# Attention's rows turned one step later, with a fourth place for rows, and head 0's operands loaded ahead of a weight tile

## What is computed

```python
proj = u @ w_in                                  # xp | q | k | v | gate_logits
z = einsum('bhqd,bhkd->bhqk', qb, kb) * scale    # 8 heads of 64, 8 query blocks of 128
mask = kpos < qpos
log_beta = log_sigmoid(z)
log_1m_beta = where(mask, log_sigmoid(-z), 0.0)
log_a = log_beta + cumsum(log_1m_beta, axis=3, reverse=True) - log_1m_beta
a = where(mask, exp(log_a), 0.0)                 # the rows of weights
out = einsum('bhqk,bhkd->bhqd', a, vb)
g = sigmoid(gate_logits)                         # gates, from u @ w_in as well
m = g_pool * y_pool + g_sb * (out @ w_branch_attn)
```

## Time and profile before

| what | us |
|---|---|
| median of 3 runs | 1917.36 (1917.35 to 1918.03) |
| the profiled execution's own time | 1918.11 |
| its span | 1916.2 |
| PE busy | 1903.5 (99%) |
| PEld busy | 1592.0 (83%) |
| DVE busy | 1372.2 (72%) |
| ACT busy | 796.4 (42%) |
| POOL busy | 115.9 (6%) |

### The profile page before, as it was taken

The page is one execution under the profiler, slowest core; times in us unless marked ns, Lnnn a source line. Parts: engine busy times, 40 slices in busy tenths (PEclk is TensorE's granted clock), DMA queues, the critical chain, the costliest instruction groups (busy, mean ns, idle before and its releaser), DMA issues.

```text
span 1916.2 us, 24977 instructions
## 1 busy us (share of the span) xinstructions
PE 1903.5 (99%) x9010; PEld 1592.0 (83%) x9010; DVE 1372.2 (72%) x1677; ACT 796.4 (42%) x1175; POOL 115.9 (6%) x157
## 2 busy tenths in 40 slices
PE   9999999999999999999999999999999999999998
PEld 8888888888888888888888888898888888888887
DVE  6978777784566776488677768889777777756555
ACT  7423232323434544234676752474323232324344
POOL 1000000000000300000233220010000000000001
PEclk9999999999999999999999999999999999999999
DMA  5456654558676733416875447643545444677665
GB/s 165 144 198 230 223 181 140 199 189 306 208 240 201 195 110 132 132 50 181 226 174 148 128 139 260 197 138 119 178 144 196 149 169 153 216 264 244 206 192 206
DMA packets 258419, 348.24 MB, mean 182 GB/s; under 512 B 29344, under 2 KB 161184, under 8 KB 255008
## 3 DMA queue, kind: packets, MB, share of 16 engines
q1 hardware_dynamic: 258336, 347.15, 56.3%
HBM read 233.83 MB, written 112.99 MB: 181 GB/s over the span
## 4 chain that ended last, share of the span: by engine, by line
PE 97%; DVE 1%; DMA 1%; issue 0%; SPq 0%; ACT 0%; POOL 0%; POOLq 0%; DVEq 0%; ACTq 0%
PE bank L1263 40%; PE bank L1372 9%; PE bank L1319 9%; PE bank L1321 9%; PE bank L1320 9%; PE bank L1513 6%; PE bank L1215 3%; PE bank L1449 2%; PE bank L1421 2%; PE bank L1479 2%; PE bank L1585 2%; PE bank L1604 1%; PE bank L1190 1%; PE bank L1603 1%; PE bank L1570 1%; PE bank L1568 1%
## 5 line engine op out<-in xcount | busy, mean ns | idle before, releaser
L2253 DVE TENSOR_TENSOR dn_lo<-dn_lo_raw,dn_hi 128x1024 fp32r<-128x1024 f32 x149 | 181.9, 1224 | 149.6 <-ACT dn_hi L1788 149.1
L1263 PE MATMUL bank<-lo_t,wa_hi 128*128 128x512 f32 x656 | 252.8, 389 | 0.0
L1263 PE MATMUL bank<-hi_t,wa_hi 128*128 128x512 f32 x656 | 252.8, 389 | 0.0
L1263 PE MATMUL bank<-hi_t,wa_lo 128*128 128x512 f32 x656 | 252.8, 389 | 0.0
L1788 ACT ACTIVATE dn_hi<-dn_lo_raw 128x1024 fp32r<-128x1024 f32 x149 | 158.0, 1061 | 218.8 <-DMA dn_lo_raw<-act_dram 218.8
L1319 PE MATMUL bank<-dn_hi 128*128 128x512 f32 x596 | 232.7, 390 | 0.0
L1321 PE MATMUL bank<-dn_lo,dn_hi 128*128 128x512 f32 x596 | 231.9, 389 | 0.0
L1320 PE MATMUL bank<-dn_hi,dn_lo 128*128 128x512 f32 x596 | 231.9, 389 | 0.0
L1263 PE MATMUL bank<-hi_b,wa_hi 128*128 128x512 f32 x492 | 190.6, 389 | 1.0 <-DVE up L2387 1.0
L1263 PE MATMUL bank<-lo_b,wa_hi 128*128 128x512 f32 x492 | 190.5, 389 | 0.0
L1263 PE MATMUL bank<-hi_b,wa_lo 128*128 128x512 f32 x492 | 190.4, 389 | 0.0
(11 more groups left out here) (275 smaller groups left out, 3747.7 us busy)
## 6 DMA issues: line engine op xcount, KB each, us to landing
wa_lo_raw<-in_ffn_w_gate_up_dram SPq DMA_DIRECT2D x87, 512.0 KB, 5.0
dn_lo_raw<-act_dram SPq DMA_DIRECT2D x149, 256.0 KB, 4.2
act_dram<-g SPq DMA_DIRECT2D x44, 512.0 KB, 4.4
wd_t<-in_ffn_w_down_dram SPq DMA_DIRECT2D x44, 512.0 KB, 6.6
act_dram<-s_of SPq DMA_DIRECT2D x88, 256.0 KB, 6.5
wd_dram<-wd_t SPq DMA_DIRECT2D x22, 1024.0 KB, 6.0
dn_lo_raw<-wd_dram SPq DMA_DIRECT2D x85, 256.0 KB, 3.4
dn_lo_raw<-in_ffn_w_down_dram SPq DMA_DIRECT2D x64, 256.0 KB, 3.0
```

Of the source, the lines that this page charges most:

```text
L1263: last = nc.tensor.matmul(acc, lhs, rhs, start=n == 0 and i != 2 and i < 5, stop=n == 11, skip_group_check=True)
L2253: return nc.vector.tensor_tensor(dst, raw, hi.bitcast(f32), ALU.subtract)
```

## The change

The lag between a tile's logits and its transposes goes from two steps to three (`LAG`), with a fourth place for rows (`a3`) and one more step at the end (`DRAIN`). The weighing of pairs moves from even to odd steps. On DVE the low halves always go before the scan. The second gate unit is loaded behind head 0 instead of before it, and its four pieces are split somewhat later.

```diff
-DRAIN = 4
+DRAIN = 5
+LAG = 3
...
-    return gate_step(piece_start(j) + (7 + 18 * piece if j < NG - 1 else 1 + 6 * piece))
+    return gate_step(piece_start(j) + (20 if j == 1 else 7) + 18 * piece if j < NG - 1 else piece_start(j) + 1 + 6 * piece)
...
+        a3 = at("a3", [P, SEQ], f32, o + 16384)
...
             gate_unit(0)
             spill_pool_branch(2)
-            gate_unit(1)
...
             load_head(0)
+            gate_unit(1)
             spill_pool_branch(3)
             load_head(1)
...
-                    if s == NA:
+                    if s == NA + 1:
                         move_o(NA // 2 - 2, 3, slice(0, HALF // 2))
-                    elif s == NA + 2:
+                    elif s == NA + 3:
                         move_o(NA // 2 - 1, 4, slice(HALF // 2, HALF))
-                    elif s >= 4 and s % 2 == 0:
-                        store_o((s - 4) // 2)
+                    elif s >= LAG + 2 and s % 2:
+                        store_o((s - LAG - 2) // 2)
...
             def weights_of(n):
-                return a2[:, :] if n % 3 == 2 else a[:, n % 3, :]
+                return (a[:, 0, :], a[:, 1, :], a2[:, :], a3[:, :])[n % 4]
...
                 gate_parts(g0, cut)
-                if s >= 4 and s % 2 == 0:
-                    weigh((s - 4) // 2)
-                if 2 <= s < NA + 2:
-                    turn(s - 2)
+                if s >= LAG + 2 and s % 2:
+                    weigh((s - LAG - 2) // 2)
+                if LAG <= s < NA + LAG:
+                    turn(s - LAG)
...
                 if n >= 2:
                     act.wait_ge(a_ok, n - 1)
-                if n >= 3:
-                    act.wait_ge(t_ok, CHUNKS[n - 2])
+                if n >= 4:
+                    act.wait_ge(t_ok, CHUNKS[n - 3])
...
-                if s >= 4 and s % 2 == 0:
-                    take_o((s - 4) // 2)
-                if 2 <= s < NA + 2:
-                    turned_hi(s - 2)
+                if s >= LAG + 2 and s % 2:
+                    take_o((s - LAG - 2) // 2)
+                if LAG <= s < NA + LAG:
+                    turned_hi(s - LAG)
...
-                turned_first = 2 <= s <= NA and TILES[s - 1]["qt"] in (1, 5, 3)
-                if turned_first:
-                    turned_lo(s - 2)
+                if LAG <= s < NA + LAG:
+                    turned_lo(s - LAG)
                 if 1 <= s <= NA:
                     weigh_keys(s - 1)
-                if 2 <= s < NA + 2 and not turned_first:
-                    turned_lo(s - 2)
```

## The result

The changed kernel takes 1926.25 us (median of 5, 1925.14 to 1927.6), the kernel before 1917.63: ratio 1.0043, 95% interval 1.0032 to 1.0055. It is 8.6 us slower, where I forecast 2.2 us less. The profiled execution took 1925.14 us with a span of 1923.2, against 1918.11 and 1916.2 before. From the first gate matmul to the first of the branch the stage takes 247.8 us instead of 240.5; nothing outside it moved by more than 0.3 us.

The account below looks back on a forecast made before the run. PE, busy 99% of the span, was taken as the bound, with only waits to win: -1.4 (pipeline) - 0.9 (head 0) + 0.1 (`pool_y`) = -2.2 us, giving a median of 1915.2 us, range 1913.3 to 1918.6.

Parts of the forecast that it names:

- That only waits can be won, and which: PE in the changed stage: no matmul is removed, so only waits count, 3.6 us in all, 1.9 at head 0.
- Head 0's wait: PE's wait for head 0's late keys: loading them ahead of the weights gains 0.9 us, bounds nothing to 1.9.
- The Trainium skill's fixed cost plus bytes: Head 0's key transfers: 2.0 us plus bytes at 436 GB/s, about 2.3 us, gaining 1.9 us; rejected for the measured row.
- What stands behind the megabyte: DMA transfers after the moved weights: about 2.2 us later, `pool_y` at 926.9, charged 0.1 us, bounds 0 to 2.
- My sign of being wrong: At POOL: its wait for `pool_y` ending later than 927.4 with PE waiting at tile 2 would show the forecast wrong.
- Who waits for the mask of tile 2: POOL's mask, then DVE's scan, 2.3 us after `pool_y` lands: tile 2's transposes, in step 5, allow landing until 927.4.
- The later pieces of the second gate unit: Splitting of the moved weights on ACT: each piece a step later, claimed covered, so no cost.
- Low halves first: DVE order before the scan: two waits before weighings within the stage go, 0.3 us gained; the scan's delay costs nothing.
- One more step at the end: The stage's tail: last turning, weighing and gates keep their distances; cost 0, bounds -0.1 to +0.3 us.
- The lag: Three steps from logits to transposes, with a fourth place: PE's waits for scanned rows go, 1.1 us gained.
- scans as the bound: Rival at DVE's loop: longer than two steps for wide tiles, late `betas` stall PE; 1921.2 us or more, chance 0.10.
- a late `pool_y`: POOL's wait for `pool_y`, with later tiles' masks queued behind it: charged 0.1 us, bounds 0 to 2 us.

## Why the prediction was wrong

- **That only waits can be won, and which.** Right. Head 0's wait was forecast to fall by 0.9 us. By starts it fell from 1.77 to 0.76 us, 1.0 us; with the 0.1 us at `q_st`, which is gone too, 1.1 us. The lines are

```profile
912.15 0.39 PE L1374 MATMUL bank<-u_hi,w_lo 128*128 128x512 f32 x1
913.14 0.50 PE L1570 MATMUL bank<-k_hi,q_st 128*128 128x512 f32 x1 [0.60 <-DMA k_lo<-qk_dram]
```

The size was nearly right, the way to it less so. The transfers of keys took 2.8 to 3.5 us from issue to landing, all of them less than the 3.8 us that I had taken as the best case, and they were issued 0.2 us earlier; but PE, too, reached the second chunk 0.3 us earlier. The Trainium skill's fixed cost plus bytes ("DMA: Bandwidth & Descriptors", "Anatomy of one DMA") would have cleared the wait. The page gives it for transfers that GpSimd issues, so it was not the rule for these, which SyncE issues; the 0.76 us that stayed agrees with the row and not with that figure.
- **What stands behind the megabyte: the step that failed.** I wrote that "all behind it lands about 2.2 us later" and that `pool_y` at 926.9 was "covered by half a microsecond". It landed near 929.2, 4.6 us later. The term was worked out from bytes in the DMA engines, 3.6 us less 1.0 and 0.5 for slack. What it left out is SyncE's own queue: the issue of `pool_y` alone moved by 3.7 us, 3.2 of them the time that issuing the weights, the stores and head 1 took, and the transfer itself took 0.9 us longer. The 1.5 us that I had taken off did not show. My sign of being wrong came as written: POOL's wait ended at 929.27, later than 927.4, and PE waited, though one weighing earlier than I had said.
- **Who waits for the mask of tile 2.** The same step named only the transposes of tile 2. On DVE, low halves first means that the scan of tile 2 in step 3 stands ahead of the low halves of tile 1 in step 4, and these are wanted by the first weighing, which PE reaches before those transposes. I priced the new order within a step and did not follow it into the next. The run with the scan moved shows the two apart: 6.2 us with this link, 1.9 us without it. The later pieces of the second gate unit were priced as covered on ACT; on DVE one of them stood in this chain, for 1.7 of the 6.2 us.
- **The clock.** Not in the forecast: a stall of 6 us brought 3.2 us at 1.2 GHz, 1.35 us more.
- **Low halves first.** "The two waits before weighings within the stage go": they did not; waits of 0.29, 0.21 and 1.35 us stand in their place. At the last, near 1074 us, DVE's rows show a split and the differences of the values, together 2.9 us, right ahead of the low halves that the weighing, now in an odd step, wants:

```profile
1070.63 1.72 DVE L3050 TENSOR_TENSOR w_lo<-w_raw,w_hi 128x512 fp32r<-128x512 f32 x1
1072.28 1.21 DVE L2943 TENSOR_TENSOR v_w_raw<-v_w_raw 128x1024 f32<-128x1024 f32 x1
1073.41 1.14 DVE L3038 TENSOR_TENSOR at_lo<-bank,at_hi 128x512 fp32r<-128x512 f32 x2
```

This place was not tested by itself. In the run with later gates its wait was 0.28 us, but a wait of 0.75 us came near 1011 us, which the changed kernel does not have, and that one went when the values were moved. The causes of the 0.29 and the 0.21 us stay open.
- **One more step at the end.** Costed at 0, bounds -0.1 to +0.3 us; it cost 0.8 us. The step has five gate matmuls and no logits, so the last pair but one lost the distance that it had before. The end itself kept its balance, as forecast: the last gate at 1156.58, the branch at 1156.93.
- **The lag.** The waits for rows did go (0.45, 0.53 and 0.11 us), as forecast.

The sum by measured terms: 6.2 for the first weighing, 1.35 for the clock, 1.35, 0.8 and 0.5 for the later waits, less 1.1 at head 0 and 1.4 for the old waits: 7.7 us. The stage grew by 7.3 us in the profiled execution; the 0.4 us between them is not accounted for. The medians are 1.6 us further apart than the profiled executions. That the landing of `pool_y`, which PE now follows, differs between executions could explain this; only the profiled executions have traces, so it is not shown.

The rival that ended on the right side, scans as the bound, had the wrong mechanism: ACT waited for a scan once in the whole stage, the 5.1 us within the stall. I had a late `pool_y` as a cost of 0 to 2 us and not as a rival; its bound above was the mistake in the chances.

## What to carry to other kernels

When a load is moved, follow every queue behind it. The issuer's own queue comes first, for issuing takes time too: here it was 3.2 of the 3.7 us by which a transfer was issued late. Then follow every in-order queue behind each waiter into the following steps: here a transfer delayed one POOL instruction, and two more engines later PE stood still. Keep instructions that wait for a DMA behind those that the critical engine wants, rather than tune the DMA's arrival; putting POOL's gates two steps later took back the whole loss. A longer lag between stages is worth only as much as the shortest distance left: here it came with a new parity of steps and a short added step, and with the gates put later, lag 2 and lag 3 came out level, 0.9996 and 0.9997. A stall can cost more than its length: the three of 2.8 to 6.1 us here were each followed by another 1.2 to 1.5 us of slow clock.

## What was not expected of the hardware

- After PE had stood for 6.1 us, its granted clock was 0.51 for 3.2 us (256 columns at 0.21 us instead of 0.12). After 4.1 us, in the run with the new load order alone, it was 0.50 for 2.7 us, and after 2.8 us, in the run with the loads put back, it fell to 0.50 as well. After 1.7 us, in the run with the scan of tile 2 moved, it stayed at 1.00. What it cost was 1.35, 1.2 and 1.5 us: the shortest of the three stalls paid no less than the longest. The Trainium skill ("TensorE: Matmul & The Clock Gate", section "Part 1: The HAM clock gate") says that the array falls to the 1.2 GHz level when it has been idle; the 0.50 and 0.51 agree.
- The same load order gave landings of `pool_y` of 924.7 and 926.2 us in two kernels, with the same issue times within 0.6 us. From issue to landing the first one took 6.0 us before the change, 6.9 in the changed kernel, 7.5 with the weights behind it and 8.2 with the loads put back. What sets this is open.
- SyncE took longer to issue the same four stores of 256 KB right behind the megabyte of weights: 4.0 us in the changed kernel and 4.3 with the new load order alone, against 2.3 before the change and with the loads put back, and 2.4 with the weights behind `pool_y`.
